# An encoder layer's attention: normalizing the outputs after the values instead of the probabilities before them

## The reference, cut to what matters

```python
s = jnp.einsum('bqkgd,bskd->bkgqs', qi, k, preferred_element_type=jnp.float32) * scale
p = jax.nn.softmax(s, axis=-1).astype(v.dtype)
return jnp.einsum('bkgqs,bskd->bqkgd', p, v)
```

## Time and profile before

| what | value |
|---|---|
| median of 3 runs | 1475.54 us |
| profiled execution | 1476.55 us |
| its span, first to last instruction | 1474.8 us |
| PE, DVE, ACT, POOL busy | 99%, 72%, 50%, 30% |
| granted TensorE clock | 1.0 throughout |
| attention stage | from about 185 to 412 us |
| POOL in the 40 slices (37 us each) | nine tenths in slices 6 to 9, with DVE at 8 to 9 and ACT at 8 to 9 |

### The profile page before, as it was taken

How to read it: one execution, slowest core, us unless ns; L and a number is a source line. 1 busy time by engine, 2 the same in 40 slices (tenths; PEclk the granted TensorE clock), 3 DMA queues, 4 the chain that set the end, 5 groups by cost and what they waited for, 6 DMA issues and landing times.

```text
span 1474.8 us, 23217 instructions
## 1 busy us (share of the span) xinstructions
PE 1465.4 (99%) x7812; PEld 1306.3 (89%) x7812; DVE 1059.2 (72%) x1310; ACT 737.0 (50%) x1267; POOL 444.0 (30%) x419
## 2 busy tenths in 40 slices
PE   9999999999999999999999999999999999999999
PEld 8999978888888889999999999999888888888887
DVE  6765799999868785544554454449887888888875
ACT  6232399999847755545555554546322322322220
POOL 3467599888935420000000000001230221311300
PEclk9999999999999999999999999999999999999999
DMA  8555330100245849333233334347644344343434
GB/s 263 149 119 118 85 106 15 29 11 11 87 146 192 291 155 378 131 142 140 103 145 135 133 114 153 119 178 281 245 158 157 100 157 132 112 154 111 135 99 183
DMA packets 89067, 209.10 MB, mean 142 GB/s; under 512 B 8240, under 2 KB 27568, under 8 KB 88880
## 3 DMA queue, kind: packets, MB, share of 16 engines
q1 hardware_dynamic: 86816, 197.27, 40.2%
q10 hardware_dynamic: 2192, 11.08, 1.8%
HBM read 129.93 MB, written 71.57 MB: 137 GB/s over the span
## 4 chain that ended last, share of the span: by engine, by line
PE 94%; ACT 1%; DVE 1%; POOL 1%; issue 1%; DMA 0%; ACTq 0%; POOLq 0%; DVEq 0%
PE ps L909 24%; PE ps L910 24%; PE ps L911 24%; PE ps L1172 6%; PE ps L1054 4%; PE ps L1182 3%; PE ps L1036 2%; PE ps L1038 2%; PE ps L1069 2%; PE ps L1070 2%; ACT prob L1386 1%; POOL prob L2478 0%; DVE pTlo L1800 0%; DMA ident<-in_ident 0%; ACT pThi L1305 0%
## 5 line engine op out<-in xcount | busy, mean ns | idle before, releaser
L909 PE MATMUL ps<-h,wuhi 128*128 128x384 f32 (+1 forms) x904 | 301.3, 333 | 0.2 <-issue 0.2
L911 PE MATMUL ps<-h,wulo 128*128 128x384 f32 (+1 forms) x904 | 301.1, 333 | 0.0
L910 PE MATMUL ps<-h,wuhi 128*128 128x384 f32 (+1 forms) x904 | 301.1, 333 | 0.0
L909 PE MATMUL ps<-wdhi,hidhi 128*128 128x512 f32 x672 | 261.6, 389 | 0.4 <-DVE yacc L2294 0.3
L910 PE MATMUL ps<-wdlo,hidhi 128*128 128x512 f32 x672 | 261.5, 389 | 0.0
L911 PE MATMUL ps<-wdhi,hidlo 128*128 128x512 f32 x672 | 261.5, 389 | 0.0
L2294 DVE TENSOR_TENSOR yacc<-yacc,ps 128x1024 f32<-128x1024 f32 x167 | 203.1, 1217 | 76.2 <-PE ps L911 76.1
L1305 ACT ACTIVATE hidhi<-hin 128x1024 fp32r<-128x1024 f32 (+1 forms) x72 | 86.8, 1206 | 301.6 <-PE ps L911 293.2
L2208 DVE TENSOR_TENSOR u<-u,ps 128x384 f32<-128x384 f32 x96 | 53.1, 553 | 180.4 <-PE ps L911 180.3
L909 PEld LDWEIGHTS ps<-h,wuhi 128*128 128x128 f32 x904 | 169.7, 188 | 0.6 <-issue 0.4
L910 PEld LDWEIGHTS ps<-h,wuhi 128*128 128x128 f32 x904 | 169.7, 188 | 0.0
(11 more groups left out here) (227 smaller groups left out, 2878.3 us busy)
## 6 DMA issues: line engine op xcount, KB each, us to landing
hd<-hout SPq DMA_DIRECT2D x64, 384.0 KB, 3.2
hin<-hd SPq DMA_DIRECT2D x48, 512.0 KB, 3.6
hd<-hout SPq DMA_DIRECT2D x32, 576.0 KB, 2.8
hin<-hd SPq DMA_DIRECT2D x24, 768.0 KB, 4.4
wuraw<-in_w_up SPq DMA_DIRECT2D x17, 1024.0 KB, 6.1
wdraw<-in_w_down SPq DMA_DIRECT2D x8, 2048.0 KB, 9.3
h<-h2d ACTq DMA_DIRECT2D x7, 1536.0 KB, 11.1
x2in<-in_x SPq DMA_DIRECT2D x12, 512.0 KB, 3.3
```

What stands on the lines that cost most here:

```text
L909: pe.matmul(out, w_hi, m_hi, start=start, stop=False, skip_group_check=resumed)
L910: pe.matmul(out, w_hi, m_lo, start=False, stop=False, skip_group_check=resumed)
L911: return pe.matmul(out, w_lo, m_hi, start=False, stop=stop, skip_group_check=resumed)
```

## The change

The exponentials are turned and multiplied with the values as they are, undivided; `transpose_p` waits for the exponentials alone. `normalize` is gone. The reciprocals are taken once for each output (4 columns) instead of once for each group. SP stores them to a DRAM tensor `rinvd` (`store_inv`), so that they come to lie as one row of 512 numbers, and loads this row into 64 partitions (`spread_inv`, rinvb). POOL multiplies each output by it after its addition. Both new functions run inside `move_out`, for the output after the one that is moved. `o_moved` is one semaphore instead of two, `o_saved` counts two for each output, and the sample's queries are rounded by POOL instead of ACT.

```diff
+            def store_inv(s, pair, idx, half):
+                n = s.out(pair, idx, half)
+                sp.wait_ge(inv_done, n + 1)
+                sp.dma_start(rinvd[bass.ds(n, 1)].rearrange("a q t -> t (a q)"),
+                             rinv[:, s.parity(pair, idx), slot_cols(s, half)], allow_slow_non_contiguous=True).then_inc(inv_stored, 16)
+            def spread_inv(s, pair, idx, half):
+                n = s.out(pair, idx, half)
+                a = (idx % 2 if s.n else half) * 64
+                sp.wait_ge(inv_stored, 16 * n + 16)
+                if not isinstance(n, int) or n >= 2:
+                    sp.wait_ge(o_saved, 2 * n - 2)
+                if not isinstance(n, int) or n:
+                    sp.wait_ge(inv_in, 16 * n)
+                row = rinvb_last if isinstance(n, int) and n == OUTS - 1 else rinvb
+                sp.dma_start(row[a:a + 64], rinvd[bass.ds(n, 1)].rearrange("a q t -> (a q t)").partition_broadcast(64)
+                             ).then_inc(inv_in, 16)
             def move_out(s, pair, idx, half):
...
+                if later:
+                    store_inv(*later)
                 sp.wait_ge(o_copied, n + 1)
-                sp.dma_start(o_part[a:a + 64], o_full[b:b + 64, half]).then_inc(o_moved[half], 16)
+                if not isinstance(n, int) or n:
+                    sp.wait_ge(o_moved, 16 * n)
+                sp.dma_start(o_part[a:a + 64], o_full[b:b + 64, half]).then_inc(o_moved, 16)
+                if later:
+                    spread_inv(*later)
+            store_inv(seqs[0], 0, 0, 0)
+            spread_inv(seqs[0], 0, 0, 0)
...
-                    pe.wait_ge(norm_done, s.group(pair, idx, (half + 1) * GRP // s.halves))
+                    pe.wait_ge(exp_done, s.group(pair, idx, (half + 1) * GRP // s.halves))
...
+                if u % (GRP // s.halves) == 0:
+                    free = slot_free(s, pair, idx, u * s.halves // GRP)
+                    if not isinstance(free, int) or free > 0:
+                        act.wait_ge(inv_done, free)
...
-                    act.wait_ge(o_saved, n - 1)
+                    act.wait_ge(o_saved, 2 * n - 3)
...
+            def inverses(s, pair, idx, half):
+                b, q = s.parity(pair, idx), slot_cols(s, half)
+                free = slot_free(s, pair, idx, half)
+                dve.wait_ge(exp_done, s.group(pair, idx, (half + 1) * GRP // s.halves))
+                if not isinstance(free, int) or free > 0:
+                    dve.wait_ge(inv_stored, 16 * free)
+                dve.reciprocal(rinv[:, b, q], rsum[:, b, q]).then_inc(inv_done, 1)
...
-            def normalize(s, pair, idx, u):
...
+                pool.tensor_scalar(blocks(Qs[a:a + 64, 2 * (idx % 2)]), qk_cols(a, pair, c0, 512), 1.0, 1.0, ALU.mult, ALU.mult
+                                   ).then_inc(q_hi, 1)
...
+                pool.wait_ge(o_saved, 2 * n + 1)
+                pool.wait_ge(inv_in, 16 * n + 16)
+                pool.tensor_tensor(att_out(a, pair, c0), att_out(a, pair, c0),
+                                   (rinvb_last if n == OUTS - 1 else rinvb)[a:a + 64].rearrange("p (s c) -> p s c", s=2), ALU.mult).then_inc(o_saved, 1)
```

More of the change, by code:

```diff
@@ L420, in inverted_in, with slot_free, slot_cols @@
         def inverted_in(s, pair, idx, k):
-            if k % 2:
-                return None
[L424 to L437, removed]
+            later = later_job(s, pair, idx, 1)
+            if not later or k not in (0, 4) or k == 0 and later[0].n:
+                return None
+            return (*later, int(k == 4 and later[0].n == 0))
+        def slot_free(s, pair, idx, half):
+            n = s.out(pair, idx, half)
+            if s.n == 0:
+                return n - 3
+            return {NQ: NQ - 3, NQ + 1: NQ - 1}[n] if isinstance(n, int) and n < NQ + 2 else n - 1
+        def slot_cols(s, half):
+            return slice(4 * half, 4 * half + 4) if s.n == 0 else slice(0, 4)
         def qk_cols(a, j, c0, n):
@@ L2470, in _, with split_q @@
             done = WINDOW_STEPS // 2
-            def normalize(s, pair, idx, u):
[L2473 to L2481, removed]
+            def split_q(s, pair, idx):
                 a, b = idx % 2 * 64, (1 - idx % 2) * 64
                 c0, m = s.start + idx // 2 * 512, s.out(pair, idx, 0) - NQ + 1
-                pool.wait_ge(norm_done, normalized)
                 if done:
                     pool.wait_ge(win_step, done)
+                pool.wait_ge(qT_in[s.n], 16 * s.len // P)
+                pool.wait_ge(s_done, GRP * (s.job(pair, idx) - 1))
+                pool.wait_ge(q_hi, NQ + m - 1)
+                pool.tensor_scalar(blocks(Qs[a:a + 64, 2 * (idx % 2)]), qk_cols(a, pair, c0, 512), 1.0, 1.0, ALU.mult, ALU.mult
+                                   ).then_inc(q_hi, 1)
                 pool.wait_ge(q_hi, NQ + m)
@@ L2492, in split_q, with add_out @@
                 pool.wait_ge(q_lo[1], m)
-            def add_out(n, normalized):
+            def add_out(n):
                 half = n % 2
@@ L2507, in add_out @@
                 pool.wait_ge(o_copied, n + 1)
[L2508 removed]
+                pool.wait_ge(o_moved, 16 * n + 16)
                 pool.tensor_tensor(att_out(a, pair, c0),
@@ L2561, in _ @@
                     for idx in range(s.per):
[L2562 to L2569, removed]
+                        nxt3 = later_job(s, pair, idx, 3)
+                        n = s.out(pair, idx, 0)
                         if n == OUTS - 2:
@@ L2572, in _ @@
                         if n and n < OUTS - 1:
-                            add_out(n - 1, min(g + GRP + 3 + bool(ahead), GROUPS_ALL))
-                        if nxt and not ahead:
-                            normalize(*nxt, 3)
+                            add_out(n - 1)
                         if nxt3 and nxt3[0].n:
-                            split_q(*nxt3, g + 2 * GRP)
+                            split_q(*nxt3)
                         if s.n == 0 and pair == 0:
@@ L2590, in _ @@
                             split_k(1, True, idx)
[L2591 to L2595, removed]
+                        if s.n == 0:
+                            add_out(n)
+                        if n == OUTS - 2:
                             split_wq(2)
```

49 lines of the change are left out of this document (21 added, 28 removed).

## The result

The changed kernel took 1517.08 us (median of 4 runs, 1513.7 to 1518.94), the kernel before 1475.39 on the same chip: a ratio of 1.028 (95% interval 1.0259 to 1.0301), 41.7 us slower. The forecast was 1483.7, range 1474 to 1493: right in sign and in its first mechanism, far off in size, and outside its range.

A forecast was written before the change was run, and what follows sets the result against it. TensorE, busy 99% of the span, was taken as the bound. A 9.4 us stall from SP's queue less 1.2 us from lighter engines gave +8.2 us, 1483.7 us against the median of 1475.54, range 1474 to 1493.

The forecast's parts named there:

- first mechanism: SP's queue: store and spread cycles delay KB, so TensorE stands before the sample's first scores, 9.4 us.
- What bounds the kernel, and where the change bites: TensorE, busy 99% of the span; the change touches only the attention stage and its cost is on SP's queue.
- The start: SP's queue: first store waits behind woraw (10.0 us, to 195.3) and lands about 3 us later, at 198.4.
- The store's finish: Reciprocals' store to DRAM: 2.6 us of finishing after its pieces move, a little above rsd's 2.2.
- The cycle: SP's queue, spread to spread: 3.7 + 1.1 + 2.6 = 7.4 us, against 5.9 between prompt outputs; ends 4.7 and 9.8.
- The spread: 2 KB row loaded into 64 partitions: nearest row rsb takes 4.7 us, engines busy until 3.7 us after issue.
- rival C: Small writes cost far more than in rsd: cycles near 10 us, o_part late too, 1493.5 or above; chance 0.14.
- Stall before the sample's first scores: TensorE waits for KB, landing at 226.8 instead of by 217.4: 9.4 us late.
- SP catches up and is hidden from there: In the sample a job takes 11.0 us, more than one SP cycle, so the transfers no longer delay TensorE.
- The engines' gain: Lighter ACT, DVE and POOL shorten TensorE's waits in the attention stage: -1.2 us, between 0 and -2.4.
- A: Transfers stay hidden, SP's cycle under 5 us, KB in time, only -1.2 us left: 1474.3; chance 0.20.
- B: Lighter engines win all 2.4 us of TensorE's waits and nothing stalls: 1473.1 or somewhat below; chance 0.04.

The follow-up runs named there:

- e1: Kernel before, with single DMAs added between the sample's outputs: stores in several layouts, a spread, a small copy alone and behind a store; 1476.57 us.
- e5: Kernel before, with single DMAs between the sample's outputs, small writes at various spacings, sizes and counts; 1475.33 us.
- e9: Kernel before, with single DMAs of small writes in different groupings and orders, and a store on ScalarE's queue ahead of SP's copy; 1479.42 us.
- e2: Changed kernel with the DRAM row's layout turned, each partition's four values side by side, POOL reading with a stride; 1476.31 us, 1.0004 to the kernel before.
- e7: Changed kernel with scattered stores and SP's wait for each landing, but no spreads and reciprocals not applied; 1515.43 us, 1.0263 to the kernel before.
- e6: Changed kernel with scattered stores, no spreads, no SP wait before the output's copy, reciprocals not applied; 1512.80 us, 1.0247 to the kernel before.
- e8: Kernel before, with TensorE held four times in the sample until 1, 2, 3 and 4 copies in a row landed; 1494.66 us against 1475.91.
- e4: Changed kernel without stores and spreads, POOL multiplying the output by itself, division by row sums left out; 1477.23 us, 1.001 to the kernel before.
- e11: Changed kernel with each partition's reciprocals side by side in DRAM, plus two POOL waits for VectorE's operations; 1473.90 us, 0.9990 to the kernel before.

## Why the prediction was wrong, step by step

- **What bounds the kernel, and where the change bites**: right. TensorE in the attention stage, through SP's queue, first by KB before the sample's first scores; SP waited for the store in each cycle.
- **The start**: the first spread was forecast for 198.4 and came at 198.46, by luck: woraw took 13.5 us from its issue at 184.18, not 10.0, and the store landed 0.8 us behind it, not 3.
- **The store's finish**, the term that failed: "I take 2.6 for the finish". It measured about 6 us in the changed kernel (pieces moved by 201.1, landed at 207.0), and 8.1 us in all for the store by itself (e1). The nearest row was rsd: 128 adjacent pieces of 8 bytes, 4.3 us. e5 puts that form at 3.0 and e1 and e9 put 128 adjacent pieces of 4 bytes at 7.5 and 8.0: the row carried a milder dose of the same effect, and I scaled it by the number of pieces, which e1 shows to be nearly free. The cycle was 8.6 to 10.8 us, not 7.4. With 1.6 for the store (e2) nothing is late.
- **The spread**: priced too high, 4.0 us in the median and 3.0 alone, where 4.7 was read off rsb and 3.7 went into the cycle. All of them together are worth some 4.6 us in the stage (e7, one execution each), none of it the first cause.
- **What stands behind the store**: not only the wait. A DMA issued after a slow store lands with it (9.5 us instead of 1.7 in e1), and in e6 held copies and slow stores, with no spreads and no wait of SP for a landing ahead of the copy, keep 28.0 of the stage's 35.9 us. The prediction had "o_part comes late too" under rival C, with no price, and held copy_out's wait to be met "several us ahead while the queue of SP keeps up". It is four of the six stalls, and POOL's late halves of the queries, behind late additions, a fifth.
- **Stall before the sample's first scores**: 9.4 us forecast; they came 15.3 us late, of which the wait for KB was 7.40 and the rest the two stalls before it and the slower clock behind them.
- **"SP catches up and is hidden from there"**: wrong until about 300 us: 3.94, 2.10 and 5.94 us in the sample; right after 310.
- **No term for the clock**: TensorE's busy time rose by 10.6 us with the same work, 1.8 for each of the six stalls, near the 1.6 of e8. With it the account closes: 24.8 us of stalls, 10.6 of slower work and 1.7 of small waits are the 37.1 us of the span.
- **The engines' gain**: -1.2 forecast, none measured (e4: +1.9 in the median, -1.1 in one execution); e11's gain of 1.6 us has two orders set right besides. VectorE was to be 8.6 us lighter; its busy time in e2 is 1059.1 us, as before (1059.2), though it ran 56 instructions less.
- **Rivals**: C, given 0.14, was what happened, with the sample's jobs reached as well; its worked 1493.5 is too small, since it, too, counted KB's lateness alone. A and B had no part in it. The fixed 2.0 us that spoke for A, the Trainium skill (DMA: Bandwidth & Descriptors, Anatomy of one DMA) gives for DMAs that GpSimd issues; these are issued by SP.
- **The warning that I had cited**: the Trainium skill (DMA: Bandwidth & Descriptors, Rules for kernel authors) asks to rearrange a strided last dimension, since it makes one descriptor per element. The remedy is right (e2), the reason doesn't carry it: 512 descriptors 64 bytes apart take 1.8 us.

Still open: why a densely filled row finishes so late, in what unit the density counts (8 bytes apart 3.0 us, 16 apart 1.4), and why 16 adjacent pieces are quick where 64 are not. Open, too, is why a stall of 2.40 us left the clock alone where one of 2.03 did not. The trace shows landings, not what the memory does. Nor is e6's loss divided further between copies held behind a store and stores that follow each other too slowly.

## What to carry to other kernels

Price a scattered store by where its pieces land, not by how many there are: let each partition write its 16 bytes or more together, and take the stride on the reading engine. Copies issued right behind a slow store, on its own queue or on another, landed with it, so follow each later transfer to the engine that waits for it. And most stalls of TensorE from 2.03 us up cost more than their length here, 1.6 to 3 us on average.

## What the hardware showed that I had not expected

- 4-byte writes of 128 partitions into one row of 512 bytes: 7.5 us; the same bytes and three times more as 16-byte pieces: 1.4.
- A copy on SP's queue, issued 0.7 us after such a store on ScalarE's, landed after 8.1 us instead of 2.2.
- VectorE's copy of 128x512 beside POOL's sum: 2.29 us instead of 0.41.
- A hold of 0.86 us left TensorE's clock at 1.00; one of 2.61 us brought it to half for a while; a stall of 2.40 us in another run did not.
